# Attention stage of an encoder kernel: another engine issues the row of maxima, the head's loads are cut in two, and the meta items' remainders change engine

## The reference

```python
def _attend_queries(q, k, v, scale):
    s = jnp.einsum('bqhgd,bkhd->bhgqk', q, k, preferred_element_type=jnp.float32) * scale
    p = jax.nn.softmax(s, axis=-1).astype(v.dtype)
    return jnp.einsum('bhgqk,bkhe->bqhge', p, v)
```

## Time and profile before

| | |
|---|---|
| time, median of 3 runs | 3834.11 us (3818.81 to 3848.44) |
| the profiled execution | 3846.59 us |
| its span, first to last instruction | 3844.7 us |
| mean granted TensorE clock | 0.959 |
| TensorE busy | 3566.2 us (93%) |
| VectorE, ScalarE, GpSimd busy | 2774.4, 2361.8, 1248.4 us |
| attention stage | about 541 to 2655 us |

### The profile page before, as it was taken

The page is one execution under the profiler, slowest core; times in us unless marked ns, Lnnn a source line. Parts: engine busy times, 40 slices in busy tenths (PEclk is TensorE's granted clock), DMA queues, the critical chain, the costliest instruction groups (busy, mean ns, idle before and its releaser), DMA issues. The chain is left out here.

```text
span 3844.7 us, 52934 instructions
## 1 busy us (share of the span) xinstructions
PE 3566.2 (93%) x16911; PEld 2864.0 (74%) x16911; DVE 2774.4 (72%) x4963; ACT 2361.8 (61%) x4291; POOL 1248.4 (32%) x1105
## 2 busy tenths in 40 slices
PE   7999969999999999999999999998999489999991
PEld 7999946667666766688888888886888468777871
DVE  5666668889888988898889888975444565555554
ACT  4444415777777777777777777787444046555554
POOL 0000000011101110288888888884000023333330
PEclk9999968999999999999999999998999689999995
DMA  4565672320232023303321332101444179999988
GB/s 167 170 218 178 215 181 83 65 57 16 63 65 61 18 57 66 63 9 63 64 49 23 64 65 45 26 9 65 149 144 147 68 222 264 264 261 262 272 240 290
DMA packets 315250, 462.30 MB, mean 120 GB/s; under 512 B 120666, under 2 KB 252022, under 8 KB 303894
## 3 DMA queue, kind: packets, MB, share of 16 engines
q1 hardware_dynamic: 256442, 367.83, 32.7%
q0 software_dynamic: 19152, 69.74, 7.8%
q10 hardware_dynamic: 39456, 22.29, 1.9%
HBM read 312.74 MB, written 146.90 MB: 120 GB/s over the span
## 5 line engine op out<-in xcount | busy, mean ns | idle before, releaser
L997 POOL TENSOR_TENSOR b_p_lo<-b_prob,b_p_hi 128x512 fp32r<-128x512 f32 x704 | 917.4, 1315 | 780.9 <-ACT b_prob L1041 776.7
L1040 ACT ACTIVATE b_p_hi<-b_psS 128x512 fp32r<-128x512 f32 (+1 forms) x1376 | 825.1, 600 | 532.2 <-PE b_psS L1232 514.2
L1232 PE MATMUL b_psS<-b_q,b_k 96*128 96x512 f32 (+3 forms) x3440 | 1069.1, 408 | 26.7 <-DMA b_q<-b_nmxT 24.9
L1041 ACT ACTIVATE b_prob<-b_psS 128x512 f32<-128x512 f32 (+1 forms) x1376 | 817.4, 594 | 0.0
L1232 PEld LDWEIGHTS b_psS<-b_q,b_k 96*128 96x128 f32 (+3 forms) x3440 | 600.1, 184 | 192.1 <-DMA b_q<-b_nmxT 27.7
L1142 DVE TENSOR_REDUCE b_mx_s<-b_psM 128x1 f32<-128x412 f32 (+1 forms) x1228 | 680.7, 581 | 68.2 <-PE b_psM L1283 58.1
L1283 PE MATMUL b_psM<-b_k,b_q 96*128 96x412 f32 (+7 forms) x1596 | 558.7, 355 | 28.8 <-DMA b_q<-QGL 21.5
L1273 PE MATMUL b_psO<-b_p_lo,b_v 128*65 128x512 f32 (+1 forms) x1280 | 509.0, 398 | 0.4 <-POOL b_p_lo L997 0.4
L1110 DVE TENSOR_TENSOR b_p_lo<-b_prob,b_p_hi 128x512 fp32r<-128x512 f32 x576 | 420.3, 736 | 67.9 <-ACT b_prob L1041 59.9
L1125 DVE TENSOR_TENSOR b_acc<-b_acc,b_prob 128x512 f32<-128x512 f32 (+1 forms) x592 | 409.9, 692 | 46.0 <-ACT b_prob L1041 29.8
L1283 PEld LDWEIGHTS b_psM<-b_k,b_q 96*128 96x128 f32 (+1 forms) x1596 | 304.8, 191 | 138.9 <-DVE b_mx_s L1142 33.1
(11 more groups left out here) (271 smaller groups left out, 5906.2 us busy)
## 6 DMA issues: line engine op xcount, KB each, us to landing
e_first_w_gu<-w_gate SPq DMA_DIRECT2D x17, 1024.0 KB
e_first_w_gu<-w_up SPq DMA_DIRECT2D x17, 1024.0 KB
e_first_w_dn<-w_down SPq DMA_DIRECT2D x17, 1024.0 KB
e_w_gu<-w_gate SPq DMA_DIRECT2D x17, 1024.0 KB
e_w_gu<-w_up SPq DMA_DIRECT2D x17, 1024.0 KB
e_w_dn<-w_down SPq DMA_DIRECT2D x17, 1024.0 KB
a_x_raw<-xallT SPq DMA_DIRECT2D x25, 512.0 KB, 5.3
a_x<-xall SPq DMA_DIRECT2D x25, 512.0 KB, 4.3
```

The lines of the kernel that those rows point to most:

```text
L997: nc.gpsimd.tensor_tensor(p_lo[:, slot, :], prob[:, slot, :], p_hi[:, slot, :].bitcast(F32), ALU.subtract).then_inc(lo_ready, 1)
L1040: nc.scalar.activation(p_hi[0:kn, slot, :], psS[0:kn, j % 2, :], ACT.Exp)
L1041: nc.scalar.activation(prob[0:kn, slot, :], psS[0:kn, j % 2, :], ACT.Exp).then_inc(p_ready, 1)
L1232: m = nc.tensor.matmul(psS[0:kn, j % 2, :], kk[s][0:r, k], qq[s][0:r, q], start=n == 0, stop=n == len(passes) - 1)
```

## The change

ScalarE issues the row's DMA, behind item 80 of each head (`ROW_AT + 1`), in place of SyncE. Part "s" of the loads is cut in two. Part "u" holds `q0`, `k0` and the meta keys: six DMAs, issued where part "s" was. SyncE then waits for the row's landing (`row_loaded`) and only then issues the rest of "s": `q1`, `k1` and the raw values (three DMAs in GQA heads, five in MLA heads). New semaphores `ld_u` tell TensorE's maxima units that "u" is there; a wait for all of "s" is added before item 0 of the next head. At the stage's start the loads of head 1 are cut at the row of head 0 in the same way. Apart from that, the remainders of the meta items go from VectorE to GpSimd, with a drain ahead of and behind each.

```diff
-            per_gqa, per_mla = (9, 11) if part == "s" else (8, 10)
+            per_gqa, per_mla = {"u": (6, 6), "s": (3, 5), "p": (8, 10)}[part]
...
-            def row(n, s, gqa):
-
-                sp.wait_ge(row_made, n + 1)
-                dst = q1[s][GD:GD + 1, :] if gqa else q0[s][QKD:QKD + 1, :]
-                sp.dma_start(dst.bitcast(F32).rearrange("o (a b) -> o a b", b=P), nmxT[:, :].bitcast(F32)).then_inc(row_loaded, 16)
-                sp.wait_ge(row_loaded, 16 * n + 16)
-                sp.sem_inc(carrier, 1)
...
-            for s in range(2):
-                load(s, 0, s, True, "s")
-                load(s, 0, s, True, "p")
-            row(0, 0, True)
+            load(0, 0, 0, True, "s")
+            load(0, 0, 0, True, "p")
+            load(1, 0, 1, True, "u")
+            sp.wait_ge(row_loaded, 16)
+            sp.sem_inc(carrier, 1)
+            load(1, 0, 1, True, "s")
+            load(1, 0, 1, True, "p")
...
                     sp.wait_ge(pv_done, h * NI + SAMPLE_LAST + 1 + NP)
+                    load(h + 2, i + 1, s, kind, "u")
+                    sp.wait_ge(row_loaded, 16 * h + 32)
+                    sp.sem_inc(carrier, 1)
                     load(h + 2, i + 1, s, kind, "s")
-                row(h + 1, 1 - s, nxt)
...
@@ GpSimd
-                if META_ITEM[j] or not on_pool(gqa, j):
+                slot = slot_of(h, j)
+                if META_ITEM[j]:
+                    pool.wait_ge(p_ready, h * NI + j + 3)
+                    pool.drain()
+                    nc.gpsimd.tensor_tensor(p_hi[M_LO, slot, :], prob[M_HI, slot, :], p_hi[M_HI, slot, :].bitcast(F32),
+                                            ALU.subtract).then_inc(meta_lo_ready, 1)
+                    pool.drain()
                     return
...
@@ ScalarE
+            def row(n, s, gqa):
+
+                act.wait_ge(row_made, n + 1)
+                dst = q1[s][GD:GD + 1, :] if gqa else q0[s][QKD:QKD + 1, :]
+                act.dma_start(dst.bitcast(F32).rearrange("o (a b) -> o a b", b=P), nmxT[:, :].bitcast(F32)).then_inc(row_loaded, 16)
...
+            row(0, 0, True)
...
                     exp(h, s, gqa, j)
+                    if not last and j == ROW_AT + 1:
+                        row(h + 1, 1 - s, nxt)
...
@@ VectorE
-                if META_ITEM[j]:
-                    meta_rest(h, s, j)
...
@@ TensorE
-                    pe.wait_ge(ld_s[1 - s], loads_seen(i1, nxt, "s"))
+                    pe.wait_ge(ld_u[1 - s], loads_seen(i1, nxt, "u"))
...
+                    pe.wait_ge(ld_s[1 - s], loads_seen(i1, nxt, "s"))
                     pe.wait_ge(row_loaded, 16 * h + 32)
```

More of the change, by code:

```diff
@@ L752, in stage_attend @@
         ld_p = [sem("prompt_loaded0"), sem("prompt_loaded1")]
+        ld_u = [sem("unit_loaded0"), sem("unit_loaded1")]
         first_s, first_p = sem("first_sample_loaded"), sem("first_prompt_loaded")
@@ L894, in load @@
             def load(h, i, s, gqa, part):
-                if part == "s":
-                    q, k, sm = slice(SEQ, TOK), slice(SAMPLE, KEYS), ld_s[s]
+                if part == "p":
+                    q, k, sm = slice(0, SEQ), slice(0, SAMPLE), ld_p[s]
                 else:
-                    q, k, sm = slice(0, SEQ), slice(0, SAMPLE), ld_p[s]
+                    q, k, sm = slice(SEQ, TOK), slice(SAMPLE, KEYS), ld_u[s] if part == "u" else ld_s[s]
                 def dma(dst, src):
@@ L905, in load @@
                     rq, rk = bass.ds(h * GD, GD), bass.ds(i * GD, GD)
-                    if h > 0:
+                    if h > 0 and part != "s":
                         dma(q0[s][0:GD, q], t["QGH"][rq, q])
@@ L910, in load @@
                         dma(k0[s][GD:P, k], t["KGH"][rk, k])
-                        if part == "s":
+                        if part == "u":
                             dma(k0[s][0:GD, META_S:KT], t["KGH"][rk, 0:META])
                             dma(k0[s][GD:P, META_S:KT], t["KGH"][rk, 0:META])
-                    dma(q1[s][0:GD, q], t["QGH"][rq, q])
-                    dma(k1[s][0:GD + 1, k], t["KGL"].rearrange("g r n -> (g r) n")[bass.ds(i * (GD + 1), GD + 1), k])
+                    if part != "u":
+                        dma(q1[s][0:GD, q], t["QGH"][rq, q])
+                        dma(k1[s][0:GD + 1, k], t["KGL"].rearrange("g r n -> (g r) n")[bass.ds(i * (GD + 1), GD + 1), k])
                     vh = i
@@ L919, in load @@
                     rk, rr = bass.ds(m * ND, ND), bass.ds(m * RD, RD)
[L920 to L930, removed]
+                    if part != "s":
+                        dma(q0[s][0:ND, q], t["QNH"][rk, q])
+                        dma(q0[s][ND:QKD, q], t["QRH"][rr, q])
+                        dma(k0[s][0:ND, k], t["KMH"][rk, k])
+                        dma(k0[s][ND:QKD + 1, k], t["KRH"][:, k])
+                        if part == "u":
+                            dma(k0[s][0:ND, META_S:KT], t["KMH"][rk, 0:META])
+                            dma(k0[s][ND:QKD + 1, META_S:KT], t["KRH"][:, 0:META])
+                    if part != "u":
+                        dma(q1[s][0:ND, q], t["QNL"][rk, q])
+                        dma(q1[s][ND:QKD, q], t["QRL"][rr, q])
+                        dma(k1[s][0:ND, k], t["KML"][rk, k])
+                        dma(k1[s][ND:QKD, k], t["KRL"][:, k])
                     vh = m + Q_PAIRS
+                if part == "u":
+                    return
                 vcol = bass.ds(vh * VC, VD)
@@ L957, in _ @@
             sp.wait_ge(cleared, 1)
-            sp.sem_inc(ld_s[0], 16 * 6)
+            sp.sem_inc(ld_u[0], 16 * 6)
             sp.sem_inc(ld_p[0], 16 * 4)
-            for s in range(2):
-                load(s, 0, s, True, "s")
-                load(s, 0, s, True, "p")
-            row(0, 0, True)
+            load(0, 0, 0, True, "s")
[5 more added lines that the diff above has]
+            load(1, 0, 1, True, "p")
             for name in MIX_PARTS:
@@ L991, in remainder @@
             def remainder(h, s, gqa, j):
-                if META_ITEM[j] or not on_pool(gqa, j):
+                slot = slot_of(h, j)
[5 more added lines that the diff above has]
+                    pool.drain()
                     return
-                slot = slot_of(h, j)
+                if not on_pool(gqa, j):
+                    return
                 pool.wait_ge(p_ready, h * NI + j + 3)
@@ L1095, in _ @@
         def _(dve):
[L1096 to L1099, removed]
             def split(h, s, j):
-                if on_pool(True, j) and not META_ITEM[j]:
+                if META_ITEM[j] or on_pool(True, j):
                     return
                 dve.wait_ge(p_ready, h * NI + j + 3)
-                if META_ITEM[j]:
-                    meta_rest(h, s, j)
-                    return
                 slot = slot_of(h, j)
```

## The result

Over nine runs of each kernel the median goes from 3829.3 to 3808.5 us, 20.9 us less; the ratio is 0.9946 with a 95% interval of 0.9928 to 0.9964. The time forecast was 3791 from a median of 3834.1, a gain of 42.9 us. About half came. The profiled execution's span went from 3844.7 to 3812.1 us.

The account below looks back on a forecast made before the run. TensorE was taken as the bound inside heads, with row waits and low clock at boundaries; 23.5 + 17.9 + 2 + 0.5 - 0.5 - 0.5 = 42.9 us off 3834.1 gave 3791 us, 8-in-10 range 3771 to 3820.

Parts of the forecast that it names:

- The stall and the clock: At head boundaries: TensorE's whole wait for the row goes, 23.5 us, and the low clock behind it, 17.9 us.
- The meta remainders in GQA heads: In GQA heads: VectorE's relief outweighs GpSimd's holds, 2 us gained; bounds 5 gained and 17 lost.
- The meta remainders in MLA heads: In MLA heads: VectorE's relief gains 0.5 us, GpSimd's added work loses 0.5, with bounds 0 and 9 for the loss.
- Rival 1: At head boundaries: the row's issue holds ScalarE, exponentials stop, TensorE stalls; 43 us slower, 3877; chance 0.06.
- Rivals 2 and 3: At boundaries: row still late, gain 20, 3814, chance 0.12; or low clock not the stall's, gain 25, 3809, chance 0.06.
- Rival 4: VectorE and GpSimd's shared resource costs 17 us in GQA heads, 9 in the last; 15 us gained, 3819; chance 0.08.

Follow-up runs that it names:

- e1: The changed kernel with the meta remainders back on VectorE in all heads, keeping the cut loads and ScalarE's row; 3793.5 us, ratio 0.9892 to the kernel before.
- e8: e1 with the meta remainders of the GQA heads left out, VectorE still making those of the MLA heads; ratio 0.9905 to the kernel before.
- e7: e1 plus an unused GpSimd subtraction of 16 x 512, with drains, at the meta items of the GQA heads; ratio 0.9952 to the kernel before.
- e5: The changed kernel with GpSimd making the meta remainders in MLA heads only, VectorE in GQA heads; ratio 0.9907 to the kernel before.
- e3: The changed kernel with part "s" of the loads uncut, ScalarE issuing the row, meta remainders on VectorE; ratio 0.9939 to the kernel before.
- e4: The changed kernel with loads cut but SyncE issuing the row between the parts, meta remainders on VectorE; ratio 0.9893 to the kernel before.
- e2: The kernel before with only the meta remainders moved to GpSimd, old loads and row kept; ratio 1.0007 to the kernel before.
- e6: e5 with head 1's loads uncut at the stage's start and SyncE's wait for the row's landing there gone; ratio 0.9899 to the kernel before.
- e12: e5 with all GQA remainders on VectorE, head 1 loaded whole and SyncE's wait for the first row kept; 3780.0 us, ratio 0.9868.

## Why the prediction was right, and where its size was off

**The stall and the clock** were right in mechanism and size: 41.4 us forecast, 41.4 in e1. ScalarE's issue of 0.79 us came as worked out, SyncE went on 2.3 us behind it, and part "u" was nearly through by then: the DMA traffic falls from 153 GB/s in 1091:1092 to 15 in 1092:1093. One reading was loose: the eight stalls "of about 2 us or more" have one of 1.75 us among them (at 978.8), and that lies in the span where the clock fell in some executions and not in others. So this part of the clock's term could have come out smaller in another execution.

**The meta remainders in GQA heads** are the term that was mis-sized, and with the wrong sign: 2 us gained was taken, with 17 lost as the far bound, and 14.4 us were lost in heads 2 to 8 (e1 against the change), 2.1 a head. The first head is 5.0 us longer too, of which about 3.0 are low clock (14.7 us of it against 8.7) and 2.1 the same hold. So the meta remainders cost about 16.5 us in the eight heads, close to the far bound of 17. The working had the price of a hold at 0.36 us (0.5 was measured) and set it against 0.68 us of relief in one sum of VectorE's time. That was the error: TensorE doesn't feel VectorE's sum, it feels how late the next two maxima are. The relief came where VectorE had room and was worth nothing (e8); the hold came at the three meta items beside which maxima run and cost 14.4 / 21 = 0.69 us at each, 0.88 in e7. The earlier trace rows had shown such a hold, though none of TensorE's waits lies behind that one. All of the 12 waits end 2.4 us behind the start of a GpSimd remainder (the first of them at 635.03, GpSimd's start at 632.65); I read them as the bound of what VectorE could cost and not as what a GpSimd instruction costs where maxima are due.

**The meta remainders in MLA heads**: 0 net was taken (0.5 gained, 0.5 lost), 5.3 us came by the change against e1, 3.7 by e5 against e1. VectorE's instruction there lasted 1.04 us in the mean, from 0.68 to 1.84 with a GpSimd instruction beside every one, where it is 0.68 throughout in the GQA heads; without it the weight loads' waits fell from 6.4 to 1.4 us. GpSimd had the room that the slack gave it, in the last head too: its new instruction took 1.29 us where 1.6 were estimated, and TensorE waited 0.4 us in all for a remainder of GpSimd (window 1750:2625).

**Rivals.** Rival 1, ScalarE held by its issue, did not come even with all of part "s" queued (e3). Rivals 2 and 3 did not come. Rival 4, with a chance of 0.08, came for its GQA part, and the measured 3808 lies between its 3819 and the forecast's 3791. The 0.55 given to a gain of over 1% did not come. The rule quoted in the prediction from the Trainium skill ("DMA: Bandwidth & Descriptors", section Issuing engines are not separate DMA queues) was read as: another issuer gives nothing. e4 bears that out; e3 shows that it is too strict, as there the other issuer gave 18.6 us in a kernel whose loads weren't cut.

**What stays open.** Of the sum, 41.4 - 14.4 - 5.0 + 5.3 = 27.3 us is the attention's gain in the traces; the runs' medians show 20.9. The difference is of the size of the scatter of the other stages and was not traced to a cause. A part of it may be the trace of the kernel before itself: its granted clock is 0.959, where the median of the 18 executions of that kernel in e1's session is 0.961, and 0.002 of 3830 us is 8 us. Then the typical execution had less low clock to give back than rows 8 show, and the prediction, which took the same gain off the median as off the profiled execution, took it too large.

## What to carry to other kernels

Where one engine's short stalls decide, don't add up the busy time of the engine that it waits for: ask which of its instructions is late at the place of the wait, and what a neighbour that can hold it up does there. A transfer that is needed soon wants few bytes queued ahead of it; cutting the loads around it gave all, and the other queue two thirds in heads 2 to 8 when the loads stayed whole. A cost tried on a kernel that still has a stall behind it may hide in the stall (e2: 3.7 us instead of 14.4): take the stall out first, then price the rest. And a wait that is removed from a queue also lets go what stands behind it (e6: 4 MB of weights).

## What the runs showed of the hardware

- GpSimd's remainder of 16 x 512 takes as long as its remainder of 128 x 512: 1287 and 1288 ns, in the MLA heads of the kernel after (window 1750:2500).

```profile
L1007 POOL TENSOR_TENSOR b_p_lo<-b_prob,b_p_hi 128x512 fp32r<-128x512 f32 x460 | 587.6, 1288 | 86.1 <-ACT b_prob L1051 77.7 <-issue 3.7
L1000 POOL TENSOR_TENSOR b_p_hi<-b_prob,b_p_hi 16x512 fp32r<-16x512 f32 x35 | 45.0, 1287 | 6.5 <-ACT b_prob L1051 3.8 <-issue 2.7
```

- GpSimd's instruction does not hold every instruction of VectorE. Held are the remainders, which have both inputs in SBUF: 0.68 us alone, up to 1.84 beside GpSimd. Not held are the adds of the denominator in the MLA heads, whose sum lies in PSUM, though GpSimd is busy 656 of the 750 us of the window 1750:2500: the longest takes 0.70 us. The maxima, read from PSUM, take 0.58 us beside GpSimd and alone.

```profile
L1134 DVE TENSOR_TENSOR b_acc<-b_acc,b_prob 128x512 f32<-128x512 f32 x392 | 271.4, 692 | 14.6 <-ACT b_prob L1051 4.9 <-issue 3.4
```

- The hold goes both ways. In the GQA heads of the kernel after (window 727:1570) 34 of GpSimd's 40 instructions of 16 x 512 take 1.28 to 1.29 us and six 1.82; of its ordinary remainders the 14 that began while a remainder of VectorE ran took 1.55 us in the mean, the 12 that began with VectorE idle 1.29.
- A DMA issue of SyncE lasted 5.0 to 8.7 us behind SyncE's own nine to eleven loads, while ScalarE's issue of the same row amid the same loads lasted 0.78 to 0.85 us (e3).
- Of the stalls at the head boundaries of the kernel before, e2 and e3, all of 1.9 us and over were followed by 3.4 or 6.8 us at the 1.2 GHz level; of those of 1.75 to 1.84 us two were (1.75 before, 1.76 in e3) and three were not (1.81 and 1.84 in e2, 1.75 in e3). No length of a stall settles it by itself: in the first head, a stall of 2.69 us in e1 (until 609.4) left the clock at 1.00, and one of 1.67 us in e12 (until 608.9) was followed by 3.4 us at 0.50.
